# Expert down weights as one 4 MB transfer in 32 KB pieces, and their operand turned by half-identity products

## Chip, cores and metric

One core of a Trainium2 chip runs the whole kernel. The metric is the device time of one execution in microseconds, median of several; lower is better.

## The reference, cut to what matters

One encoder layer over 384 tokens (256 prompt frames and 8 x 16 sample frames) of width 2048, all in f32: an adaLN projection, a combined input projection, sliding-window attention beside gated linear attention, an output projection, and then a mixture of experts, in which the change lies. Each token goes to 2 of 32 experts with a hidden width of 512:

```python
def expert_block(args):
    xblk, e = args
    return (jax.nn.silu(xblk @ w_eg[e]) * (xblk @ w_eu[e])) @ w_ed[e]
```

`w_eg[e]` and `w_eu[e]` are 2048 x 512, `w_ed[e]` is 512 x 2048; each is 4 MB, so an expert has 12 MB and all of them 384 MB. Every expert's weights are read once, whatever its number of tokens. Each token's row is the sum of its two experts' results with their gates; it is scaled, added to x and normalised at the end.

## The kernel before, in words

The engines run programs of their own and meet at counting semaphores. Everything is written out by hand; the order on each engine is the order of its text.

**The ring.** Weights go through `ring`, 12 units of 8 KB per partition (1 MB each). For an expert, units 0 to 3 hold the gate weights, 4 to 7 the up weights, 8 to 11 (from `PRE` = 8) the down weights. SP loads them in six transfers of two units (2 MB, `unit_pair`), in the order gate, up, down (`expert`, L413 to L430). Each waits until `unit_used` says that TensorE has used the same two units of the expert before: TensorE adds 1 to it for each unit. A partition gets one contiguous piece of 16 KB in each transfer: `eg_v`, `eu_v` (8 neighbouring rows of 2 KB) and `ed_v` (`c=2`: two neighbouring rows of 8 KB). Expert 0's up units are requested early (L436), its gate and down units as the stages before leave the ring.

**An expert on TensorE** (`two_experts`, two experts per turn of the loop, buffers by `u`): `up(u, e)` takes the gate and the up product (L1260), in units 0 to 7, each f32 product on a half of the columns (`64 * q`), for 64 slots; it waits for `loaded[j]` at each pair of units (`expert_landed`). Then `rows_T` (L1243) turns the gathered rows of expert e + 1 by eight transposes; it waits for their gather. `hidden_T` (L1269) turns the hidden values of expert e by two 128 x 128 transposes into `bank[4]`, and ScalarE copies them to `hidT` (L1573, in `y_copy`). `down(u, e)` (L1283) takes the down product in units 8 to 11, 8 products of 512 columns for each two units, and adds 1 to `unit_used` after each unit. In this profile a product is two records.

**Beside it.** ScalarE computes the exponential of the gate, VectorE the rest of SwiGLU (L2057 to L2060); both copy the turned rows out of PSUM (L1561, L2052) and, after the down product, its result to `ysb` (L1576, L2065). GpSimd (`expert_rows`) waits for that copy, issues the scatter of expert e's result rows (L637, to `y_rows`), and then the gather of the rows of expert e + 2 (L632, into `xg`, read by `rows_T` one expert ahead). Both are indirect DMAs on GpSimd's own queue, one after the other, of 4 KB rows, 128 to a DMA; slots that hold no token are out of bounds and move nothing. They run on the same 16 DMA engines as the weights. After the last expert, `y_rows` is read back and the final norm follows.

An expert's hidden feature f lies in `hid` at partition (q, slot), f = 256 q + position. `hidden_T` before takes every second position (c = 0, 1), so that the partition p of unit 8 + 2q + c meets the weight row 256 q + 2p + c. This is the part that depends on how the rows of `w_ed` lie over the partitions.

Of the kernel before, what the change touches and what calls it, by code (L numbers as in the profile page):

```python
# [20 lines left out]
P = 128  # L21
D = 2048
# [8 lines left out]
NE, GRP, EPG = 32, 4, 8  # L31
# [10 lines left out]
PRE = 8  # L42
# [5 lines left out]
U_MOE = U_OUT + 16  # L48
UE = 12
# [52 lines left out]
def encoder_step(nc, A, O):  # L102
    with ExitStack() as ctx:
# [7 lines left out]
        ring = sb("ring", [P, RING * D])  # L111
        xbuf = sb("xbuf", [P, NT * D])
        hbuf = sb("hbuf", [P, KC * TOK])
# [11 lines left out]
        ident = sb("ident", [P, P])  # L125
# [24 lines left out]
        bank = [ctx.enter_context(nc.psum_tensor(f"bank{i}", [P, QN], F32)) for i in range(8)]  # L150
# [9 lines left out]
        def unit_pair(s):  # L160
            return ring[:, s * D:(s + 2) * D]

        arena = ring[:, PRE * D:RING * D]
        x = xbuf[:, :].rearrange("p (t d) -> p t d", t=NT)
        vr = xbuf[:, :].rearrange("p (a t c) -> p a t c", a=2, t=NT)
# [73 lines left out]
               for u in range(2)]  # L239
        ysb = [zbuf[:, 4096 + 1024 * u:5120 + 1024 * u] for u in range(2)]  # L240
        sg = [hbuf[:, 256 * u:256 * u + 256] for u in range(2)]
        hid = [hbuf[:, 512 + 256 * u:768 + 256 * u] for u in range(2)]
        hidT = [hbuf[:, 1024 + 256 * u:1280 + 256 * u].rearrange("p (c q s) -> p c q s", c=2, q=2)
                for u in range(2)]
        gfin = hbuf[:, 2048:4096]
        yk = [ring[:, 4096 * t:4096 * t + 4096].rearrange("p (k d) -> p k d", k=2) for t in range(NT)]
# [3 lines left out]
        loaded = [sem(f"loaded{s}") for s in range(RING)]  # L250
        unit_used, ada_used = sem("unit_used"), sem("ada_used")
# [46 lines left out]
        out_v = w_out.rearrange("(k p) c -> p k c", p=P)  # L298
        eg_v = A["w_expert_gate"][0].rearrange("e (g p c) f -> p e g (c f)", g=2, c=8)
        eu_v = A["w_expert_up"][0].rearrange("e (g p c) f -> p e g (c f)", g=2, c=8)  # L300
        ed_v = A["w_expert_down"][0].rearrange("e (q p c) d -> p e q (c d)", q=2, c=2)
        st_v = A["state_gla"][0].rearrange("b h k v -> b k h v")
        so_v = O["gla_state_sample"][0].rearrange("b h k v -> b k h v")
        yout = [O["y_prompt"][0, 0:P, :], O["y_prompt"][0, P:2 * P, :],
# [40 lines left out]
        def _(sp):  # L345
# [41 lines left out]
            for g in range(4):  # L387
                for j in range(8):
                    m, u = j // 4, j % 4
# [6 lines left out]
            for i in range(28):  # L396
                n = U_T + i
# [15 lines left out]

            def expert(e, first):

                for j in (0, 2, 8, 10) if first else range(0, UE, 2):
                    if first:
                        if j < 4:
                            last = max(n for n in range(U_MOE) if w_slot(n) in (j, j + 1))
                            sp.wait_ge(unit_used, last + 1)  # L420
                        elif j == PRE:
                            sp.wait_ge(h2_v, 12)
                            sp.wait_ge(h2_out[1], 16)
                        else:
                            sp.wait_ge(h2T_ps, 8)
                            sp.wait_ge(h2_out[0], 16)
                    else:
                        sp.wait_ge(unit_used, U_MOE + UE * (e - 1) + j + 2)
                    half_v = (eg_v, eu_v, ed_v)[j // 4][:, bass.ds(e, 1), j % 4 // 2, :]
                    sp.dma_start(unit_pair(j), half_v.rearrange("p e f -> p (e f)")).then_inc(loaded[j], 16)  # L430

            for j in (4, 6):
# [10 lines left out]
            with sp.If(n_over > 0):  # L443
                with sp.Fori(0, n_over) as i:
                    e = sp.value_load(ov_i[0:1, bass.ds(i + 1, 1)], min_val=0, max_val=NE - 1)
                    for j in range(0, UE, 2):
                        sp.wait_ge(unit_used, U_MOE + UE * (NE - 1) + UE * i + j + 2)
                        half_v = (eg_v, eu_v, ed_v)[j // 4][:, bass.ds(e, 1), j % 4 // 2, :]
                        sp.dma_start(unit_pair(j), half_v.rearrange("p e f -> p (e f)")).then_inc(loaded[j], 16)
            with sp.Else():  # L450
                sp.nop()
# [253 lines left out]
        def _(pe):  # L705
# [538 lines left out]
                last.then_inc(eT_ps, 1)  # L1244

            def expert_landed(j, e):
                j -= j % 2
                pe.wait_ge(loaded[j], 16 * loads[j] + 16 + e * 16)

            def up(u, e, t_need):  # L1250
# [13 lines left out]

            def hidden_T(u, e):
                pe.wait_ge(hid_sb, e + 1)
                units = hid[u].rearrange("p (n c) -> p c n", c=2)
                for c in range(2):
                    last = tr(bank[4][:, c * P:(c + 1) * P], units[:, c, :], ident[:, :])  # L1269
                last.then_inc(hT_ps, 1)  # L1270

            def down(u, e):

                pe.wait_ge(hT_sb, e + 1)
                if isinstance(e, int) and e == 0:
                    pe.wait_ge(ov_rdy, 1)
                wait_count(pe, y_v, e)
                wait_count(pe, y_a, e)
                for k in range(4):
                    expert_landed(8 + k, e)  # L1280
                    for n in range(2):
                        for q in range(2):
                            last = mm(bank[5 + n][64 * q:64 * q + 64, :], hidT[u][:, k % 2, k // 2, :],  # L1283
                                      unit(8 + k)[:, 1024 * q + QN * n:1024 * q + QN * n + QN],
                                      start=(k == 0), stop=(k == 3))
                    last.then_inc(unit_used, 1)
# [26 lines left out]
        def _(act):  # L1313
# [256 lines left out]

            def y_copy(u, e, sct_need):
                act.wait_ge(hT_ps, e + 1)
                cp(hidT[u].rearrange("p c q s -> p (c q s)"), bank[4][:, 0:256]).then_inc(hT_sb, 1)  # L1573
                act.wait_ge(unit_used, U_MOE + UE + e * UE)
                wait_count(act, sct[u], sct_need)
                cp(ysb[u][:, QN:2 * QN], bank[6][:, :]).then_inc(y_a, 1)  # L1576
# [610 lines left out]
```

## Time and profile before

| | us |
|---|---|
| median of 3 runs | 1856.45 (1856.37 to 1859.54) |
| the profiled execution, its own time | 1859.65 |
| its span | 1858.0 |
| TensorE busy | 1562.1 (84%) |
| VectorE, ScalarE, GpSimd busy | 393.5, 201.3, 181.9 |
| moved by DMA | 610.93 MB, mean 329 GB/s |
| 64 transfers each of gate, up and down weights, median to landing | 25.3, 26.7, 22.9 |

How to read it: the span is the time between the first and the last instruction of the profiled execution; its own time is the device's, and lies a little above. The expert stage runs from about 817 us, where the first gate product starts, to 1792 us. In the timeline, a row's number in brackets is how long the engine stood idle before it, and what released it.

### The profile page before, as it was taken

Reading aid. Unit: us, or ns where it says so; the run is one execution under the profiler, and the core shown is the slowest. Engines: PE = TensorE matmul, PEld = TensorE weight load, DVE = VectorE, ACT = ScalarE, POOL = GpSimd, SP = SyncE. Lnnn points to the kernel's source line nnn. Section 1 sums busy time; section 2 is a strip of 40 time slices with the busy share of each in tenths; the row PEclk is TensorE's granted clock in tenths of the full one; section 3 lists DMA queues with packets and bytes.
Section 4 is the critical chain, followed back from the end, with each engine's and each line's share of the span. In section 5 each row is a group of like instructions: output and inputs, shape, how many; then the busy total and the mean of one; then the engine's idle time right before and its main releaser. Section 6 shows DMA issues by size and latency. Waiting matters only on the chain.

```text
span 1858.0 us, 21570 instructions
## 1 busy us (share of the span) xinstructions
PE 1562.1 (84%) x8849; PEld 806.4 (43%) x8849; DVE 393.5 (21%) x852; ACT 201.3 (11%) x504; POOL 181.9 (10%) x372
## 2 busy tenths in 40 slices
PE   5999999999999999968798877777787888787840
PEld 2455444444454444554444434444444344444410
DVE  2012322224251311441111111101011111111115
ACT  3001111111221000200000000000000000000013
POOL 1031000000101020031010101010000011010102
PEclk9999999999999999978998999999989899999975
DMA  9998767666514593399999999999999999999952
GB/s 364 375 307 306 283 263 291 268 243 262 181 55 126 177 245 123 157 310 428 425 428 427 427 427 427 428 426 424 426 421 423 422 427 425 426 423 426 419 220 93
DMA packets 101954, 610.93 MB, mean 329 GB/s; under 512 B 15949, under 2 KB 18109, under 8 KB 65929
## 3 DMA queue, kind: packets, MB, share of 16 engines
q1 hardware_dynamic: 84242, 562.29, 74.8%
q0 software_dynamic: 16848, 41.68, 7.4%
q10 hardware_dynamic: 816, 6.29, 0.8%
q8 instruction: 34, 0.56, 0.1%
q14 instruction: 14, 0.11, 0.0%
HBM read 603.03 MB, written 28.40 MB: 340 GB/s over the span
## 4 chain that ended last, share of the span: by engine, by line
PE 49%; DMA 43%; DVE 3%; POOL 1%; issue 1%; ACT 1%; SPq 0%; POOLq 0%; DVEq 0%; ACTq 0%
DMA ring<-in_w_expert_up 36%; PE bank L823 9%; PE bank L1123 7%; PE bank L819 7%; PE bank L1260 6%; DMA zbuf<-h_rows,cur 5%; PE bank L1283 3%; PE bank L777 3%; PE bank L764 3%; PE bank L1150 2%; PE bank L743 1%; PE bank L768 1%; DMA ring<-in_w_ada 1%; DMA ring<-in_w_in 1%; DVE ring L2152 1%
## 5 line engine op out<-in xcount | busy, mean ns | idle before, releaser
L1260 PE MATMUL bank<-ring,zbuf 128*64 128x256 f32 x4096 | 464.2, 383 | 84.2 <-DMA ring<-in_w_expert_up 75.3
L1260 PEld LDWEIGHTS bank<-ring,zbuf 128*64 128x64 f32 x4096 | 291.5, 138 | 264.7 <-DMA ring<-in_w_expert_up 95.8
L1283 PE MATMUL bank<-ring,hbuf 128*64 128x512 f32 x1024 | 269.0, 685 | 17.6 <-ACT hbuf L1573 17.6
L823 PE MATMUL bank<-ring,hbuf 128*128 128x512 f32 x384 | 174.2, 599 | 2.9 <-ACT xbuf L1366 2.6
L1283 PEld LDWEIGHTS bank<-ring,hbuf 128*64 128x64 f32 x1024 | 82.3, 158 | 184.6 <-issue 182.7
L819 PE MATMUL bank<-hbuf,ring 128*128 128x384 f32 x384 | 133.8, 495 | 1.2 <-ACT zbuf L1362 0.8
L1123 PE MATMUL bank<-ring,zbuf 128*128 128x512 f32 x288 | 127.0, 595 | 3.1 <-DVE ring L1881 1.9
L2057 DVE TENSOR_SCALAR hbuf<-hbuf 128x256 f32<-128x256 f32 x32 | 9.4, 294 | 524.7 <-ACT hbuf L1565 524.7
L823 PEld LDWEIGHTS bank<-ring,hbuf 128*128 128x128 f32 x384 | 70.2, 190 | 83.7 <-issue 82.7
L819 PEld LDWEIGHTS bank<-hbuf,ring 128*128 128x128 f32 x384 | 69.8, 190 | 52.5 <-issue 11.0
L641 POOL CAST cur<-stab 128x1 int32 (+1 forms) x32 | 5.8, 181 | 861.5 <-DVE zbuf L2065 861.5
L1243 PE MATMUL bank<-ident,zbuf 128*128 128x128 f32 x264 | 43.2, 313 | 51.4 <-DMA zbuf<-h_rows,cur 51.4
L1123 PEld LDWEIGHTS bank<-ring,zbuf 128*128 128x128 f32 x288 | 53.7, 190 | 68.8 <-issue 68.7
L2065 DVE COPY zbuf<-bank 128x512 f32<-128x512 f32 x32 | 22.1, 692 | 286.8 <-PE bank L1283 286.8
L1565 ACT ACTIVATE hbuf<-bank 128x256 f32<-128x256 f32 x32 | 12.3, 384 | 523.1 <-PE bank L1260 523.1
L1243 PEld LDWEIGHTS bank<-ident,zbuf 128*128 128x128 f32 x264 | 35.2, 198 | 65.2 <-DMA zbuf<-h_rows,cur 60.6
L777 PE MATMUL bank<-ring,dbuf 128*32 128x512 f32 x512 | 59.1, 596 | 0.0
L2058 DVE RECIPROCAL hbuf<-hbuf 128x256 f32<-128x256 f32 x32 | 56.1, 1753 | 1.1
L1269 PE MATMUL bank<-ident,hbuf 128*128 128x128 f32 x64 | 17.9, 369 | 45.1 <-DVE hbuf L2060 45.0
L764 PE MATMUL bank<-hbuf,ring 128*128 128x384 f32 x128 | 50.3, 516 | 3.3 <-DMA ring<-in_w_in 3.3
L1576 ACT COPY zbuf<-bank 128x512 f32<-128x512 f32 x32 | 18.8, 586 | 275.5 <-PE bank L1283 275.5
L743 PE MATMUL bank<-ring,dbuf 128*32 128x512 f32 x256 | 39.3, 690 | 5.5 <-DMA ring<-in_w_ada 4.5
(389 smaller groups left out, 1133.4 us busy)
## 6 DMA issues: line engine op xcount, KB each, us to landing
ring<-in_w_expert_up SPq DMA_DIRECT2D x64, 2048.0 KB, 26.7
ring<-in_w_expert_gate SPq DMA_DIRECT2D x64, 2048.0 KB, 25.3
ring<-in_w_expert_down SPq DMA_DIRECT2D x64, 2048.0 KB, 22.9
ring<-in_w_ada SPq DMA_DIRECT2D x96, 1024.0 KB, 7.7
ring<-in_w_in SPq DMA_DIRECT2D x32, 1024.0 KB, 9.0
ring<-in_w_out SPq DMA_DIRECT2D x16, 1024.0 KB, 5.2
ring<-y_rows ACTq DMA_DIRECT2D x3, 2048.0 KB, 12.2
xbuf<-in_x_prompt SPq DMA_DIRECT2D x4, 1024.0 KB, 5.9
```

Source lines behind the costliest of these rows:

```text
L743: last = mm(bank[7][32 * q:32 * q + 32, :], cT[:, 4 * u + q, :], w[:, q, :], start=(u == 0), stop=(u == 3))
L764: last = mm(bank[c][:, 0:TOK], wq[:, k % 4, c * P:(c + 1) * P], hT[:, k, :], start=(k == 0), stop=(k == KC - 1))
L777: last = mm(bank[b][32 * q:32 * q + 32, :], cT[:, k, :], w[:, q * QN:(q + 1) * QN], start=(k == 0), stop=(k == KC - 1))
L819: last = mm(bank[c][:, 0:TOK], w[:, kk_, c * P:(c + 1) * P], hT[:, k, :], start=(k == 0), stop=(k == KC - 1))
L823: last = mm(bank[t][:, :], hT[:, k, t * P:(t + 1) * P], w[:, kk_, :], start=(k == 0), stop=(k == KC - 1))
L1123: last = mm(bank[3 * (b % 2) + t][:, :], zT[:, k, t * P:(t + 1) * P], w[:, i % 4, :], start=(k == 0), stop=(k == KC - 1))
L1150: last = mm(bank[3 + t][:, :], zT[:, k, t * P:(t + 1) * P], w[:, k % 4, :], start=(k == 0), stop=(k == KC - 1))
L1243: last = tr(bank[c // 4][:, (c % 4) * P:(c % 4 + 1) * P], rows[:, c, :], ident[:, :])
L1260: last = mm(bank[2 + u][64 * q:64 * q + 64, 256 * (j // 4):256 * (j // 4) + 256], xeT[u][:, k % 8, k // 8, :], w[:, kk_, 256 * q:256 * q + ...
L1283: last = mm(bank[5 + n][64 * q:64 * q + 64, :], hidT[u][:, k % 2, k // 2, :], unit(8 + k)[:, 1024 * q + QN * n:1024 * q + QN * n + QN], st ...
L2058: link(v.reciprocal(sg[u], sg[u]))
L2065: cp(ysb[u][:, 0:QN], bank[5][:, :]).then_inc(y_v, 1)
```

## The change

`ed_v` takes four neighbouring rows per partition (`c=4`), so that the down weights of an expert lie as 32 KB contiguous per partition, and one transfer loads all four units (`whole`, 4 MB). SP requests it when all 12 units of the expert before are used; it stays behind the up units in the order. `expert_landed` asks for the one semaphore before each of the four down units. Partition p of unit 8 + c now holds row 4p + c, so for hidden half q its 64 x 4 features must stand on partitions 64 q to 64 q + 63: `hidden_T` becomes eight products (4 c, 2 q) with half an identity as the moving operand, 64 columns each, with output at partition 64 q of `bank[4]`. `hidT` keeps its size and its copy. The same goes for the loop over overflowing experts.

```diff
--- before.py
+++ after.py
@@ -160,6 +160,9 @@
         def unit_pair(s):
             return ring[:, s * D:(s + 2) * D]
 
+        def whole(s):
+            return ring[:, s * D:(s + 4) * D]
+
         arena = ring[:, PRE * D:RING * D]
         x = xbuf[:, :].rearrange("p (t d) -> p t d", t=NT)
         vr = xbuf[:, :].rearrange("p (a t c) -> p a t c", a=2, t=NT)
@@ -240,7 +243,7 @@
         ysb = [zbuf[:, 4096 + 1024 * u:5120 + 1024 * u] for u in range(2)]
         sg = [hbuf[:, 256 * u:256 * u + 256] for u in range(2)]
         hid = [hbuf[:, 512 + 256 * u:768 + 256 * u] for u in range(2)]
-        hidT = [hbuf[:, 1024 + 256 * u:1280 + 256 * u].rearrange("p (c q s) -> p c q s", c=2, q=2)
+        hidT = [hbuf[:, 1024 + 256 * u:1280 + 256 * u].rearrange("p (c s) -> p c s", c=4)
                 for u in range(2)]
         gfin = hbuf[:, 2048:4096]
         yk = [ring[:, 4096 * t:4096 * t + 4096].rearrange("p (k d) -> p k d", k=2) for t in range(NT)]
@@ -298,7 +301,7 @@
         out_v = w_out.rearrange("(k p) c -> p k c", p=P)
         eg_v = A["w_expert_gate"][0].rearrange("e (g p c) f -> p e g (c f)", g=2, c=8)
         eu_v = A["w_expert_up"][0].rearrange("e (g p c) f -> p e g (c f)", g=2, c=8)
-        ed_v = A["w_expert_down"][0].rearrange("e (q p c) d -> p e q (c d)", q=2, c=2)
+        ed_v = A["w_expert_down"][0].rearrange("e (p c) d -> p e (c d)", c=4)
         st_v = A["state_gla"][0].rearrange("b h k v -> b k h v")
         so_v = O["gla_state_sample"][0].rearrange("b h k v -> b k h v")
         yout = [O["y_prompt"][0, 0:P, :], O["y_prompt"][0, P:2 * P, :],
@@ -413,7 +416,7 @@
 
             def expert(e, first):
 
-                for j in (0, 2, 8, 10) if first else range(0, UE, 2):
+                for j in (0, 2, 8) if first else (0, 2, 4, 6, 8):
                     if first:
                         if j < 4:
                             last = max(n for n in range(U_MOE) if w_slot(n) in (j, j + 1))
@@ -421,12 +424,14 @@
                         elif j == PRE:
                             sp.wait_ge(h2_v, 12)
                             sp.wait_ge(h2_out[1], 16)
-                        else:
                             sp.wait_ge(h2T_ps, 8)
                             sp.wait_ge(h2_out[0], 16)
                     else:
-                        sp.wait_ge(unit_used, U_MOE + UE * (e - 1) + j + 2)
-                    half_v = (eg_v, eu_v, ed_v)[j // 4][:, bass.ds(e, 1), j % 4 // 2, :]
+                        sp.wait_ge(unit_used, U_MOE + UE * (e - 1) + (UE if j == PRE else j + 2))
+                    if j == PRE:
+                        sp.dma_start(whole(j), ed_v[:, bass.ds(e, 1), :].rearrange("p e f -> p (e f)")).then_inc(loaded[j], 16)
+                        continue
+                    half_v = (eg_v, eu_v)[j // 4][:, bass.ds(e, 1), j % 4 // 2, :]
                     sp.dma_start(unit_pair(j), half_v.rearrange("p e f -> p (e f)")).then_inc(loaded[j], 16)
 
             for j in (4, 6):
@@ -443,9 +448,12 @@
             with sp.If(n_over > 0):
                 with sp.Fori(0, n_over) as i:
                     e = sp.value_load(ov_i[0:1, bass.ds(i + 1, 1)], min_val=0, max_val=NE - 1)
-                    for j in range(0, UE, 2):
-                        sp.wait_ge(unit_used, U_MOE + UE * (NE - 1) + UE * i + j + 2)
-                        half_v = (eg_v, eu_v, ed_v)[j // 4][:, bass.ds(e, 1), j % 4 // 2, :]
+                    for j in (0, 2, 4, 6, 8):
+                        sp.wait_ge(unit_used, U_MOE + UE * (NE - 1) + UE * i + (UE if j == PRE else j + 2))
+                        if j == PRE:
+                            sp.dma_start(whole(j), ed_v[:, bass.ds(e, 1), :].rearrange("p e f -> p (e f)")).then_inc(loaded[j], 16)
+                            continue
+                        half_v = (eg_v, eu_v)[j // 4][:, bass.ds(e, 1), j % 4 // 2, :]
                         sp.dma_start(unit_pair(j), half_v.rearrange("p e f -> p (e f)")).then_inc(loaded[j], 16)
             with sp.Else():
                 sp.nop()
@@ -1244,7 +1252,7 @@
                 last.then_inc(eT_ps, 1)
 
             def expert_landed(j, e):
-                j -= j % 2
+                j = min(j - j % 2, PRE)
                 pe.wait_ge(loaded[j], 16 * loads[j] + 16 + e * 16)
 
             def up(u, e, t_need):
@@ -1264,9 +1272,11 @@
 
             def hidden_T(u, e):
                 pe.wait_ge(hid_sb, e + 1)
-                units = hid[u].rearrange("p (n c) -> p c n", c=2)
-                for c in range(2):
-                    last = tr(bank[4][:, c * P:(c + 1) * P], units[:, c, :], ident[:, :])
+                units = hid[u].rearrange("p (n c) -> p c n", c=4)
+                for c in range(4):
+                    for q in range(2):
+                        last = mm(bank[4][64 * q:64 * q + 64, 64 * c:64 * c + 64], units[:, c, :], ident[:, 64 * q:64 * q + 64],
+                                  start=True, stop=True)
                 last.then_inc(hT_ps, 1)
 
             def down(u, e):
@@ -1280,7 +1290,7 @@
                     expert_landed(8 + k, e)
                     for n in range(2):
                         for q in range(2):
-                            last = mm(bank[5 + n][64 * q:64 * q + 64, :], hidT[u][:, k % 2, k // 2, :],
+                            last = mm(bank[5 + n][64 * q:64 * q + 64, :], hidT[u][:, k, :],
                                       unit(8 + k)[:, 1024 * q + QN * n:1024 * q + QN * n + QN],
                                       start=(k == 0), stop=(k == 3))
                     last.then_inc(unit_used, 1)
@@ -1570,7 +1580,7 @@
 
             def y_copy(u, e, sct_need):
                 act.wait_ge(hT_ps, e + 1)
-                cp(hidT[u].rearrange("p c q s -> p (c q s)"), bank[4][:, 0:256]).then_inc(hT_sb, 1)
+                cp(hidT[u].rearrange("p c s -> p (c s)"), bank[4][:, 0:256]).then_inc(hT_sb, 1)
                 act.wait_ge(unit_used, U_MOE + UE + e * UE)
                 wait_count(act, sct[u], sct_need)
                 cp(ysb[u][:, QN:2 * QN], bank[6][:, :]).then_inc(y_a, 1)
```

## Rows read from the trace of the kernel before

**Rows 1.** The page: the span in 40 slices, GB/s of the DMA engines, and the chain that ended last

```profile
GB/s 364 375 307 306 283 263 291 268 243 262 181 55 126 177 245 123 157 310 428 425 428 427 427 427 427 428 426 424 426 421 423 422 427 425 426 423 426 419 220 93
...
DMA ring<-in_w_expert_up 36%; PE bank L823 9%; PE bank L1123 7%; PE bank L819 7%; PE bank L1260 6%; DMA zbuf<-h_rows,cur 5%; PE bank L1283 3%; PE bank L777 3%; PE bank L764 3%; PE bank L1150 2%; PE bank L743 1%; PE bank L768 1%; DMA ring<-in_w_ada 1%; DMA ring<-in_w_in 1%; DVE ring L2152 1%
```

**Rows 2.** Windows: length, busy us (instructions) of each engine, PEclk, DMA share, GB/s

```profile
0.00:100.00 100.00, 80.84 (x429) 38.82 (x433) 18.73 (x42) 20.53 (x34) 6.70 (x40) 0.97 1.02 371
...
850.00:852.00 2.00, 2.00 (x22) 1.26 (x18) 0.00 (x0) 0.00 (x0) 1.76 (x4) 1.00 1.03 442
...
1000.00:1200.00 200.00, 157.54 (x1130) 85.70 (x1126) 28.77 (x41) 12.82 (x27) 17.57 (x37) 0.96 1.01 427
1200.00:1400.00 200.00, 156.58 (x1118) 83.15 (x1116) 25.79 (x37) 12.16 (x25) 19.66 (x42) 0.97 1.00 425
```

**Rows 3.** Waits of TensorE, 860 to 1060 us: total, times, longest

```profile
PE bank L1243 <- DMA zbuf<-h_rows,cur: 27.1, 7, 5.0
...
PE bank L1260 <- DMA ring<-in_w_expert_up: 1.3, 1, 1.3
```

**Rows 4.** Waits of TensorE, 1080 to 1780 us

```profile
PE bank L1260 <- DMA ring<-in_w_expert_up: 71.5, 42, 2.4
...
PE bank L1243 <- DMA zbuf<-h_rows,cur: 11.6, 9, 2.4
```

**Rows 5.** Timeline of TensorE: start, us, instructions; last pair of up units, experts 13 and 31

```profile
1221.62 3.67 PE L1260 MATMUL bank<-ring,zbuf 128*64 128x256 f32 x32 [1.92 <-DMA ring<-in_w_expert_up]
...
1773.84 3.67 PE L1260 MATMUL bank<-ring,zbuf 128*64 128x256 f32 x32 [1.82 <-DMA ring<-in_w_expert_up]
```

**Rows 6.** Timeline of TensorE, 840 to 1046 us, the early experts

```profile
840.45 7.84 PE L1283 MATMUL bank<-ring,hbuf 128*64 128x512 f32 x32 [0.52 <-ACT hbuf L1573]
...
866.88 1.97 PE L1243 MATMUL bank<-ident,zbuf 128*128 128x128 f32 x8 [4.77 <-DMA zbuf<-h_rows,cur]
...
868.65 0.63 PE L1269 MATMUL bank<-ident,hbuf 128*128 128x128 f32 x2
...
869.80 8.52 PE L1283 MATMUL bank<-ring,hbuf 128*64 128x512 f32 x32 [0.52 <-ACT hbuf L1573]
...
1045.31 5.22 PE L1283 MATMUL bank<-ring,hbuf 128*64 128x512 f32 x12 [0.54 <-ACT hbuf L1573]
```

**Rows 7.** Timeline of SP and GpSimd, 801 to 852 us, their DMA issues

```profile
801.34 0.80 SPq L430 DMA_DIRECT2D ring<-in_w_expert_down  x2
...
844.90 3.77 SPq L430 DMA_DIRECT2D ring<-in_w_expert_down  x2
...
849.79 1.03 POOL L637 DMA_INDIRECT y_rows<-zbuf,cur  x1 [0.23 <-issue]
...
851.44 1.05 POOL L632 DMA_INDIRECT zbuf<-h_rows,cur  x1 [0.15 <-issue]
851.94 3.77 SPq L430 DMA_DIRECT2D ring<-in_w_expert_gate  x2
```

**Rows 8.** DMA issues and us to landing: 844:850, 849:853, 1755:1761, 1790:1800

```profile
ring<-in_w_expert_down SPq DMA_DIRECT2D x2, 2048.0 KB, 13.0
...
y_rows<-zbuf,cur POOLq DMA_INDIRECT x1, 10.2
zbuf<-h_rows,cur POOLq DMA_INDIRECT x1, 15.4
...
ring<-in_w_expert_down SPq DMA_DIRECT2D x2, 2048.0 KB, 24.1
...
y_rows<-zbuf,cur POOLq DMA_INDIRECT x1, 2.9
```

**Rows 9.** DMA queues, 1500 to 1760 us: packets, MB, share

```profile
q0 software_dynamic: 2336, 3.37, 3.5%
```

**Rows 10.** Timeline, the last expert: SP's issue and the down product

```profile
1755.61 3.77 SPq L430 DMA_DIRECT2D ring<-in_w_expert_down  x2
...
1782.26 9.67 PE L1283 MATMUL bank<-ring,hbuf 128*64 128x512 f32 x32 [0.54 <-ACT hbuf L1573]
```

## The prediction

> **What bounds the kernel now.** I read the stages first. From slice 18 of 40 on, the page's row of GB/s stands at about 427, and the longest item in the chain of waits is the landing of expert weights [rows 1]. The windows say the same: between 1000 and 1400 us the DMA engines are busy for 1.00 of the time at 425 to 427 GB/s, while TensorE is busy for 157 of 200 us [rows 2]. The expert stage is about half of the span and all of the change lies in it.
>
> Then I asked whether the weights set the pace in all of it. The waits of TensorE say no. Between 860 and 1060 us it waits 27.1 us in 7 waits for gathered rows (`rows_T`, L1243) and 1.3 us for weights [rows 3]. Between 1080 and 1780 us it is the other way: 71.5 us before the up products alone for weights, 11.6 us for rows [rows 4]. So there are two regimes. Expert 0's weights lie in the ring before its rows exist, so TensorE starts with a full ring and paces itself; it is a little faster than the DMA engines and catches up with them after some seven experts.
>
> The two paces. While the weights bind, TensorE reaches the last pair of up units at 1221.62 us and, 18 experts later, at 1773.84 us: 552.2/18 = **30.68 us an expert** [rows 5]. While TensorE paces itself, the down product starts at 869.80 and at 1045.31 us, six experts apart: 175.5/6 = **29.25 us** [rows 6]. The margin is only 1.4 us.
>
> What the 29.25 us hold: the down product of expert 0 ends at T = 840.45 + 7.84 = 848.3. GpSimd issues the scatter at 849.79 and the next gather at 851.44, on one queue [rows 7]. They land 10.2 and 15.4 us later, the gather thus at 866.8 [rows 8]; `rows_T` starts at 866.88, having waited 4.77 us, and the down product follows at 869.80 [rows 6]. The loop is down product, scatter, gather, `rows_T`, `hidden_T`, down product. **The gather's landing sets it**, not arithmetic: up(e) is finished when it comes.
>
> What makes the gather slow. Alone on idle DMA engines the last scatter lands 2.9 us after its issue; beside the weights it takes 10.2 [rows 8]. The 7.3 us between are time given to weight pieces. One 16 KB piece takes 16 x 16384 B / 427 GB/s = 0.614 us on its engine [rows 2], so some 12 weight pieces pass. Sixteen gathers and scatters make 2336 packets on the software queue [rows 9]: 2336/16 DMAs/16 engines = 9 an engine for each. So about one weight piece passes before each small packet, and a few more in front of the first.
>
> **The change, part by part.**
>
> *One 4 MB transfer.* Each engine gets 8 pieces of 32 KB (8 partitions) where it had 16 of 16 KB. The bytes are the same: 9.82 us at 427 GB/s. SP issues one DMA fewer, which is worth nothing: a transfer issued 24.1 us before it lands [rows 8] isn't held by its issue.
>
> *The later issue.* Today the halves of down(e+1) are issued when half and all of down(e) are used: 844.90 and 848.3 (two issues in 3.77 us) [rows 7]. After, both go at the end. Queued behind that wait on SP are the gate units of the next expert, whose own condition comes 3.5 us after that (851.94, [rows 7]), so they lose nothing. Does the queue run dry? The pair lands on average 13.0 us after issue [rows 8]. With one taking 4.9 us and the issues 3.4 apart, they land at about 857.2 and 862.0, so the first began near 851: the new issue at 848.5 and some 1.5 us of start are in time, by under 1 us. Price of this part alone: 0 to 2 us, once; I take 0. The first expert's merged wait costs nothing, since both halves are issued there within 0.8 us (two issues at 801.34, [rows 7]).
>
> *The down product waits for all of its weights.* In the steady state they land about 2 us after `hidden_T` is done; TensorE makes it up in the gate product, since it waits 71.5/42 = 1.7 us before each pair of up units [rows 4]. At the end the last pair, issued at 1755.61 and 3.4 us later [rows 10], lands on average 24.1 us after issue [rows 8], so both by about 1784; the last down product starts at 1782.26. Cost 0 to 2 us; with the next part I take 1.
>
> *`hidden_T` as eight half-identity products.* Two transposes take 0.63 us while TensorE paces itself [rows 6]. Every f32 product shows as two records (4096 for 2048), so eight make 16. At most they run at the pace of the 128*64 records of L1260, 3.67/32 = 0.115 us [rows 5]: 1.84 us and a pipe end of 0.3, so +1.5. At least they stream a quarter of that column count: 16 x 0.03 + 0.3, so +0.2. I take **+0.9 us**. It lies in the loop above; the copy by ScalarE behind it keeps its size. While the weights bind it is hidden by their pace (30.68 against 30.15 us); without that cover it counts in full, and so it stands in the sum.
>
> *The 32 KB piece beside the gather.* No row shows one. If it can't be interrupted, each one ahead of or between the small packets holds them 0.61 us longer. When TensorE paces itself the down transfer is issued 0.2 us after T, the scatter 1.5 us and the gather 3.1 us after T, so they run together. All eight delay the chain: 8 x 0.61 = 4.9 us. None: 0. Some are gone before the scatter's first packet stands in the queue: I count one for the 1.3 us between the issues, one under way and one for the start of the software queue, and take five: **+3.1 us**.
>
> **The sum.** 29.25 + 0.9 + 3.1 = 33.25 us an expert. That is more than 30.68, so TensorE never catches up; the DMA queue runs empty before each down product ends, the next down transfer starts with it, and it meets the scatter and gather again. What was a phase of seven experts holds for all. From the end of the first down product (848.3 + 0.9) 31 experts take 31 x 33.25 = 1030.8 us, ending at 1880.0; before it was 1782.26 + 9.67 = 1791.9 [rows 10]. The difference is 88 us. What follows keeps its length. The profiled execution took 1859.65 us, 3.2 over the median of the runs, 1856.45; the sum becomes 1948 against the first and **1945 us** against the median.
>
> A rule of the Trainium skill ("DMA: Bandwidth & Descriptors", section "Queues, rings and completion order") bears on the five: it says that an engine takes turns between its queues by whole packets of some 9 to 17 descriptors and not by single ones. By it one expert transfer's share on an engine would be one turn, which is the first rival below. No row read here shows the order of single packets; the sum goes by single pieces (+3.1 us an expert), by the page's rule it would be +4.9.
>
> **The rivals.**
>
> *A turn is a whole transfer.* Each engine would finish all eight pieces of a transfer before it serves the other queue. The 7.3 us of the scatter are 1.5 shares of 4.9 us, which doesn't speak against it. The share of the down transfer becomes 9.8 us, the gather is later by the full 4.9, the loop is 35.05 us, and the end is 0.9 + 31 x 35.05 - 943.6 = +144 us: 2000 us.
>
> *The piece isn't carried as 32 KB* (the change does not do what it says), or small packets pass through it. Then the loop is 29.25 + 0.9 = 30.15 us, still below 30.68, the weights bind again, later than before, and only the end shows: 0.9 + 1 and at most 1 for the start, 1859 us. The point between this and the forecast is a delay of the gather by 0.5 us an expert. For it: no row has a piece above 16 KB. Against it: 16 KB pieces are not passed through.
>
> *Faster.* Longer pieces move faster and the gather isn't late. Place: the down transfer. In short windows the engines reach 442 GB/s [rows 2]; a down transfer at that rate would take 9.49 us for 9.82, 31 x 0.33 = 10 us less, with 2.5 given back at the ends: 1849 us. It decides from 436 GB/s on (0.2 us an expert, 6.2 in all: 2.5 for the ends and 3.7 to be seen). For it: the first 100 us, with pieces of 2 KB mostly, show 371 GB/s at full engines. That is 2 KB in 88 ns and 16 KB in 614, so about 13 ns a piece beside its bytes. But 8 pieces fewer give only 0.1 us an expert, 3 us in all. Against it: the delay of the gather must then stay under 0.5 us.
>
> **Chances.** The forecast's mechanism 0.70, with an own range of 1904 (31.95 us: +0.3 and +2.4) to 1990 (34.7 us: +1.5 and +3.95). The whole turn 0.05, no delay 0.17, faster 0.08. A measurement of this kernel can tell 0.2% (3.7 us) from no change. The third case divides into 0.12 within that and 0.05 beyond it: faster 0.08, same 0.12, slower 0.80. The range reaches from 1858 (takes in the case without delay) to 1990; it leaves out the whole turn, the faster case and some tails, not over 0.2.
>
> **What would show it.** If right: waits of L1243 for gathered rows in nearly every expert, 7 to 9 us each, to the end; waits of L1260 for weights gone; the down product starting every 33 us; the gather landing after 17 to 19 us and the down transfer after 12 to 13, for 24.1 in the steady state; windows at 1000 to 1400 us with a DMA share near 0.92 and about 393 GB/s. `hidden_T` alone shows in L1269: 1.2 to 1.8 us. Wrong: a DMA share that stays 1.00 and an expert every 30.7 us (no delay), or every 35 us (whole turn); packets that don't fall by 128 an expert (no 32 KB pieces); a share of 1.00 with more than 436 GB/s (faster). If the gather is late but L1269 is short, the 0.9 was the wrong term; if TensorE catches up after more experts, the five pieces were too many.

## The result and the profile after

The changed kernel takes 1940.01 us (median of 4 runs, 1935.6 to 1943.5) against 1857.66 for the kernel before in the same comparison: ratio **1.044, 95% interval 1.0419 to 1.046**, slower. Forecast were 1945 us and a range of 1858 to 1990. The two profiled executions took 1940.11 and 1859.65 us, 80.5 apart, and nearly all of it lies in the expert stage: the last down product ends at 1863.72 + 8.78 = 1872.5 us, where it ended at 1791.9 [rows 10].

The page of the changed kernel: DMA busy tenths and GB/s by slice, then the two large queues (packets, MB, share of 16 engines).

```profile
DMA  9998767757224853799999999899999999999952
GB/s 366 382 297 312 282 261 282 282 226 260 84 73 146 256 150 152 266 363 387 398 383 388 403 382 407 368 410 376 411 372 394 386 397 390 390 412 394 405 203 108
...
q1 hardware_dynamic: 79634, 562.29, 72.4%
q0 software_dynamic: 16848, 41.68, 7.0%
```

The bytes are the same, and the slices that stood at 427 GB/s [rows 1] now lie between 368 and 412. The weight queue has 84242 - 79634 = 4608 packets fewer: 32 x 128 weight pieces and 32 x 16 completion packets. The 32 KB pieces are real (a transfer adds 16 small packets to its pieces, here called completion packets; the run with one late transfer below shows them alone). The chain that ended last:

```profile
DMA zbuf<-h_rows,cur 27%; PE bank L1293 15%; PE bank L831 9%; PE bank L1131 7%; PE bank L827 6%; PE bank L1251 3%; PE bank L785 3%; PE bank L772 2%; PE bank L1158 2%; PE bank L1278 2%; PE bank L751 1%; DVE zbuf L2075 1%; PE bank L776 1%; POOL y_rows L645 1%; DMA ring<-in_w_ada 1%
```

Its longest item was the landing of expert weights, 36% [rows 1]; now it is the landing of gathered rows. Windows (as in [rows 2]):

```profile
1000.00:1200.00 200.00, 154.42 (x1104) 85.89 (x1104) 27.16 (x39) 11.56 (x24) 16.77 (x36) 0.85 0.94 393
1200.00:1400.00 200.00, 155.21 (x1104) 86.09 (x1104) 25.83 (x37) 11.56 (x24) 16.78 (x36) 0.85 0.94 393
```

The DMA engines have 6% of idle time where they had none, 393 GB/s for 427 [rows 2]. Waits of TensorE from 860 to 1060 us, then from 1080 to 1860 us:

```profile
PE bank L1251 <- DMA zbuf<-h_rows,cur: 42.8, 6, 8.2
```

```profile
PE bank L1251 <- DMA zbuf<-h_rows,cur: 155.4, 23, 7.9
PE bank L1293 <- ACT hbuf L1583: 12.6, 23, 0.5
```

No wait for weights is left in the later stage, where there were 42 before up products [rows 4]. The wait for gathered rows, 27.1/7 = 3.9 us on average in the early experts and nearly gone later (11.6 us in 9 waits) [rows 3, 4], is now 42.8/6 = 7.1 us in the early and 155.4/23 = 6.8 us in the later ones. One turn of the loop, with the down products of experts 1, 30 and 31 around it:

```profile
877.44 7.09 PE L1293 MATMUL bank<-ring,hbuf 128*64 128x512 f32 x32 [0.47 <-ACT hbuf L1583]
...
1237.21 1.97 PE L1251 MATMUL bank<-ident,zbuf 128*128 128x128 f32 x8 [6.79 <-DMA zbuf<-h_rows,cur]
...
1239.11 1.23 PE L1278 MATMUL bank<-ident,hbuf 128*64 128x64 f32 x16
...
1240.88 9.63 PE L1293 MATMUL bank<-ring,hbuf 128*64 128x512 f32 x32 [0.55 <-ACT hbuf L1583]
...
1250.35 13.98 PE L1268 MATMUL bank<-ring,zbuf 128*64 128x256 f32 x128
...
1250.56 0.33 SPq L432 DMA_DIRECT2D ring<-in_w_expert_down  x1
...
1252.29 1.01 POOL L645 DMA_INDIRECT y_rows<-zbuf,cur  x1 [0.32 <-issue]
...
1253.92 1.04 POOL L640 DMA_INDIRECT zbuf<-h_rows,cur  x1 [0.15 <-issue]
...
1271.05 1.98 PE L1251 MATMUL bank<-ident,zbuf 128*128 128x128 f32 x8 [6.72 <-DMA zbuf<-h_rows,cur]
...
1835.28 9.39 PE L1293 MATMUL bank<-ring,hbuf 128*64 128x512 f32 x32 [0.55 <-ACT hbuf L1583]
...
1863.72 8.78 PE L1293 MATMUL bank<-ring,hbuf 128*64 128x512 f32 x32 [0.55 <-ACT hbuf L1583]
```

From 877.44 to 1835.28 us are 29 experts: **33.03 us an expert**, where there were 29.25 in the early phase and 30.68 later [rows 5, 6]. The order can be read off: the down product ends at about 1250.4, the 4 MB transfer is requested at 1250.56, the scatter at 1252.29, the gather at 1253.92; the gate and up products are done at 1264.3, and TensorE stands idle for 6.7 us until the rows are there. DMA issues from 860 to 1800 us, median us to landing:

```profile
ring<-in_w_expert_down SPq DMA_DIRECT2D x28, 4096.0 KB, 13.1
...
y_rows<-zbuf,cur POOLq DMA_INDIRECT x28, 13.3
zbuf<-h_rows,cur POOLq DMA_INDIRECT x28, 17.2
```

The down weights land 13.1 us after their request, as the pair did in the early experts before (13.0 [rows 8]); the gather takes 17.2 us and the scatter 13.3.

The packets that start in short windows show how the two queues share the engines: around this turn's request from 1249.5 to 1251.4 us, then from 1251.4 to 1256.9 and from 1257.65 to 1262 us; last, the kernel before from 1243.9 to 1252 us, beside its scatter and gather.

```profile
DMA packets 1, 0.00 MB, mean 0 GB/s; under 512 B 1, under 2 KB 1, under 8 KB 1
...
q1 hardware_dynamic: 64, 2.10, 101.3%
...
q1 hardware_dynamic: 51, 1.67, 89.0%
q0 software_dynamic: 50, 0.15, 8.6%
...
q1 hardware_dynamic: 216, 3.13, 90.7%
q0 software_dynamic: 213, 0.35, 11.5%
```

In the changed kernel the weight queue is empty when the down transfer is requested. Then 64 pieces of 32 KB start, four an engine, before the first packet of the scatter, though the scatter was issued at 1252.29. From there on the queues take turns nearly one for one, single weight pieces against single small packets: 51 to 50 with 32 KB pieces, 216 to 213 in the kernel before.

### The profile page after: what moved, and what is told of

It is laid out like the page before. It is cut to its first block, busy times and chain, and to the rows that moved or that the text cites. A ratio compares the mean times of both kernels' runs of the same rounds, so it can differ in the third digit from the quotient of the medians.

```text
span 1938.5 us, 22372 instructions
## 1 busy us (share of the span) xinstructions
PE 1603.9 (83%) x9297; PEld 848.7 (44%) x9297; DVE 395.3 (20%) x852; ACT 201.8 (10%) x504; POOL 181.0 (9%) x372
## 3 DMA queue, kind: packets, MB, share of 16 engines
q1 hardware_dynamic: 79634, 562.29, 72.4%
## 4 chain that ended last, share of the span: by engine, by line
PE 58%; DMA 29%; DVE 4%; POOL 3%; issue 3%; ACT 1%; SPq 0%; POOLq 0%; DVEq 0%
DMA zbuf<-h_rows,cur 27%; PE bank L1293 15%; PE bank L831 9%; PE bank L1131 7%; PE bank L827 6%; PE bank L1251 3%; PE bank L785 3%; PE bank L772 2%; PE bank L1158 2%; PE bank L1278 2%; PE bank L751 1%; DVE zbuf L2075 1%; PE bank L776 1%; POOL y_rows L645 1%; DMA ring<-in_w_ada 1%
## 5 line engine op out<-in xcount | busy, mean ns | idle before, releaser
L1268 PE MATMUL bank<-ring,zbuf 128*64 128x256 f32 x4096 | 449.1, 380 | 0.8 <-DVE zbuf L2062 0.8
L1293 PE MATMUL bank<-ring,hbuf 128*64 128x512 f32 x1024 | 280.7, 710 | 17.4 <-ACT hbuf L1583 17.4
L1251 PE MATMUL bank<-ident,zbuf 128*128 128x128 f32 x264 | 64.1, 421 | 217.0 <-DMA zbuf<-h_rows,cur 217.0
L1251 PEld LDWEIGHTS bank<-ident,zbuf 128*128 128x128 f32 x264 | 51.1, 219 | 231.7 <-DMA zbuf<-h_rows,cur 231.7
L2075 DVE COPY zbuf<-bank 128x512 f32<-128x512 f32 x32 | 22.1, 691 | 314.9 <-PE bank L1293 314.9
L785 PE MATMUL bank<-ring,dbuf 128*32 128x512 f32 x512 | 59.1, 596 | 0.0
L2062 DVE COPY zbuf<-bank 128x512 f32<-128x512 f32 x33 | 22.8, 691 | 174.0 <-PE bank L1251 174.0
L1586 ACT COPY zbuf<-bank 128x512 f32<-128x512 f32 x32 | 18.7, 585 | 287.4 <-PE bank L1293 287.4
L1571 ACT COPY zbuf<-bank 128x512 f32<-128x512 f32 x33 | 19.3, 586 | 273.9 <-PE bank L1251 273.9
## 6 DMA issues: line engine op xcount, KB each, us to landing
ring<-in_w_expert_down SPq DMA_DIRECT2D x32, 4096.0 KB, 13.1
```

The lines of the kernel that those rows point to most:

```text
L785: last = mm(bank[b][32 * q:32 * q + 32, :], cT[:, k, :], w[:, q * QN:(q + 1) * QN], start=(k == 0), stop=(k == KC - 1))
L1251: last = tr(bank[c // 4][:, (c % 4) * P:(c % 4 + 1) * P], rows[:, c, :], ident[:, :])
L1268: last = mm(bank[2 + u][64 * q:64 * q + 64, 256 * (j // 4):256 * (j // 4) + 256], xeT[u][:, k % 8, k // 8, :], w[:, kk_, 256 * q:256 * q + ...
L1293: last = mm(bank[5 + n][64 * q:64 * q + 64, :], hidT[u][:, k, :], unit(8 + k)[:, 1024 * q + QN * n:1024 * q + QN * n + QN], start=(k == 0) ...
L2075: cp(ysb[u][:, 0:QN], bank[5][:, :]).then_inc(y_v, 1)
```

## The experiments

All ran beside the kernel before; ratios are to it, with 95% intervals. The code of an edit is cut to its core. The changed kernel was run once more, unchanged: 1942.48 us, 1.0433 (1.0415 to 1.045), DMA share 0.94 again.

> The changed kernel once more, unchanged, beside the run above on the same chip: 1935 to 1943 us, loop 33.0 us.

### Only the size of a piece

The 4 MB as two transfers of 2 MB, requested together at the late moment. Each takes two of the four rows of every partition, so a piece is 16 KB.

```diff
-sp.dma_start(whole(j), ed_v[:, bass.ds(e, 1), :]...).then_inc(loaded[j], 16)
+for h in range(2):
+    sp.dma_start(unit_pair(j + 2 * h), ed_v[:, bass.ds(e, 1), 2 * D * h:2 * D * (h + 1)]...).then_inc(loaded[j], 16)
```

> The changed kernel, but the 4 MB are asked for as two 2 MB transfers of 16 KB pieces, one after the other, at the same late moment, with the same rows per partition and one semaphore. Only the size of a piece differs. Theory (32 KB pieces hold up the gather): the gather lands after 15.4 us again, the expert loop falls to 29.9 us or so, below 30.68, the weights bind again after the first experts, 1857 to 1866 us. Rival (the late request makes the weight queue run dry): no change, 1940 us, DMA share 0.93. Rival (the eight products): no change either, 1940 us.

Measured: 1866.69 us, 1.0038 (1.0023 to 1.0052). Its windows from 850 and from 1000 us, its DMA issues from 1080 to 1300 us, and TensorE's wait for rows from 860 to 1060 us:

```profile
850.00:1000.00 150.00, 123.84 (x914) 70.90 (x912) 21.29 (x30) 9.57 (x20) 14.01 (x30) 0.87 1.00 416
1000.00:1200.00 200.00, 170.54 (x1241) 95.04 (x1238) 28.14 (x39) 12.52 (x26) 19.57 (x42) 0.88 1.01 425
...
y_rows<-zbuf,cur POOLq DMA_INDIRECT x7, 10.3
zbuf<-h_rows,cur POOLq DMA_INDIRECT x7, 14.1
...
PE bank L1253 <- DMA zbuf<-h_rows,cur: 31.1, 7, 5.8
```

The gather lands after 14.1 us again, the DMA engines are full again, and some 75 of the 82 us are gone. Late request and products are all there, so without the 32 KB pieces they don't bring the loss, alone or together. Some 6 us stay: from 850 to 1000 us the queues move 416 GB/s for 427 (11 GB/s over 150 us are 1.65 MB, or 3.9 us at 427), where the early experts run at TensorE's pace with the slower products and the later request; the rest was not taken apart.

### One transfer, but 16 KB pieces

The kernel before with the down weights as one late 4 MB transfer. The old rows per partition give two separate pieces of 16 KB on each; the two transposes stay.

```diff
-sp.dma_start(unit_pair(j), half_v...)                       # two halves
+sp.dma_start(whole(j).rearrange("p (q f) -> p q f", q=2), ed_v[:, bass.ds(e, 1), :, :]...)   # "e (q p c) d -> p e q (c d)"
```

> The kernel before with one change: the down weights as one 4 MB transfer, requested when all units are used, but with the old rows per partition, so two separate pieces of 16 KB on each, and the two transposes. Theory: 1857 to 1862 us (0 to 2 us at the start, 0 to 2 us at the end), expert period 30.68 us. Rival (late request): most of the 82 us, 1920 to 1940 us. Rival (the products): 1857 us.

Measured: 1862.53 us, 1.0009 (0.9997 to 1.0021). Its windows from 850 and from 1000 us, its DMA issues from 1080 to 1300 us, and the weight queue on its page:

```profile
850.00:1000.00 150.00, 122.92 (x856) 68.04 (x854) 21.36 (x30) 9.15 (x20) 14.09 (x31) 0.89 1.01 426
1000.00:1200.00 200.00, 163.58 (x1119) 89.25 (x1116) 28.52 (x40) 11.37 (x25) 17.47 (x37) 0.86 1.00 424
...
y_rows<-zbuf,cur POOLq DMA_INDIRECT x7, 10.7
zbuf<-h_rows,cur POOLq DMA_INDIRECT x7, 14.7
```

```profile
q1 hardware_dynamic: 83730, 562.29, 74.9%
```

A 4 MB transfer of 16 KB pieces does no harm, though its share on an engine is as long as the changed kernel's: the gather lands after 14.7 us. The queue's packets fell only by the 512 completion packets. **What counts is the piece, not the transfer.** This refutes the rival by whole turns (2000 us), as do the packet counts above: a turn is a single piece. So the rule of the Trainium skill ("DMA: Bandwidth & Descriptors", "Queues, rings and completion order", turns of some 9 to 17 descriptors) doesn't describe what the gather met here.

The same split on the changed kernel's own rows, where the two pieces lie one behind the other, was joined again: 79634 packets, as in the changed kernel, and 1936.18 us, 1.041 (1.0374 to 1.0446). It tells nothing new of the pieces, only that writing a pattern in two parts doesn't cut it.

> The changed kernel, one 4 MB transfer as there, its access pattern written as two pieces of 16 KB on each partition that lie one behind the other. Theory: if the pattern is kept, packets are 16 KB (256 an expert) and the time is 1860 to 1867 us; if it is joined again, packets are 32 KB and the time is that of the changed kernel, 1940 us. Rival (one transfer of 4 MB, whatever its pieces, is one turn on each engine): 1940 us with 256 packets of 16 KB.

### Only the products

16 KB pieces in halves at the old moments; the new rows per partition and the eight products stay.

> The changed kernel with the down weights in halves of 2 MB and 16 KB pieces, requested at the old moments; the rows per partition and the eight products stay. Theory: the products cost 0.75 us an expert only while TensorE sets the pace, and 1 us at the end: 1857 to 1861 us, expert period 30.68 us in the later stage. Rival (the products): 31 x 0.75 = 23 us over the kernel before, 1880 us. Rival (late request): 1857 to 1861 too.

Measured: 1862.40 us, 1.0011 (1.0001 to 1.0021): 2 us. While the weights bind, the products are hidden. The other way round, the changed kernel with the two old transposes (it leaves out the new order of the features, so its result is another one; the amounts of work are the same):

```diff
-for c in range(4):
-    for q in range(2):
-        last = mm(bank[4][64 * q:64 * q + 64, 64 * c:64 * c + 64], units[:, c, :], ident[:, 64 * q:64 * q + 64], ...)
+for c in range(2):
+    last = tr(bank[4][:, c * P:(c + 1) * P], units[:, c, :], ident[:, :])
```

> The changed kernel with the two old transposes in place of the eight products; the down product then multiplies the wrong features (the result of the experts is left wrong, all amounts of work are the same). Theory: the products are one term of the loop, 0.6 to 0.75 us an expert: 31 times that off, 1917 to 1922 us, and the loop 32.3 to 32.5 us, still over 30.68. Rival (the products are what tips the loop over): 1857 to 1866 us. Rival (late request): as the theory.

Measured: 1910.84 us, 1.0285 (1.0266 to 1.0304); 29 us less than the changed kernel's 1940, its loop 32.07 us (906.14 to 1803.98 us, 28 experts). Its waits of TensorE from 1080 to 1760 us:

```profile
PE bank L1251 <- DMA zbuf<-h_rows,cur: 152.5, 21, 9.7
```

So the products cost 1.0 us an expert inside the loop, above the 0.6 to 0.75 expected, which makes them some 29 of the 82 us once the loop binds. They are not what tips it over: with the transposes it stays above 30.68.

### Cutting the loop

The gather one expert earlier on GpSimd, all of the change kept: behind the scatter of expert e it now fetches the rows of expert e + 3. (Cut: one more gather before the loop, one more column in its table, one more wait at its end.)

```diff
-wait_count(pool, eT_ps, 2 * i + u)
-column(gcur[:, 1 - u, :], gtab, 2 * i + (u + 1))
-gather(gcur[:, 1 - u, :], 1 - u)
+pool.wait_ge(eT_ps, 2 * i + (u + 1))
+column(gcur[:, u, :], gtab, 2 * i + (u + 2))
+gather(gcur[:, u, :], u)
```

> The changed kernel with the gather of each expert's rows one expert earlier on GpSimd (the rows of expert 1 before the loop, then those of e + 2 where those of e + 1 were; one more gather at the end, never read). 32 KB pieces, late request and eight products stay. Theory (the loop down product, scatter, gather, turned rows): the loop is cut, TensorE needs 14 + 4 + 2 + 8.5 = 28.5 to 29 us an expert, the weights bind at 30.7 and the time is 1857 to 1866 us, with no waits for gathered rows. Rival (32 KB pieces are slow for the weights themselves, or the queue runs dry at each expert): the waits go over to the weights and 1920 to 1940 us stay.

Measured: 1860.73 us, 1.0011 (0.9997 to 1.0025). Its waits of TensorE from 1080 to 1760 us, and its DMA issues from 1080 to 1300 us:

```profile
PE bank L1281 <- DVE hbuf L2074: 53.3, 22, 2.4
PE bank L1296 <- DMA ring<-in_w_expert_down: 47.1, 23, 2.6
PE bank L1271 <- DMA ring<-in_w_expert_up: 11.7, 17, 1.3
```

```profile
y_rows<-zbuf,cur POOLq DMA_INDIRECT x7, 14.9
zbuf<-h_rows,cur POOLq DMA_INDIRECT x7, 18.9
```

The gather is slower than ever, 18.9 us, and costs nothing, because nobody waits for it: the slow loop is not the slow gather alone but the gather as a link between two down products. The 32 KB pieces don't harm the weights themselves. In the kernel before, the same edit:

> The kernel before with the gather one expert earlier, and nothing else. Theory: the weights bind nearly the whole stage already, so only the end can gain: 1855 to 1861 us, same. Rival (the gather costs time in the kernel before too): 11.6 + 27 us of waits go, down to 1825 us.

Measured: 1861.55 us, 1.0007 (0.9995 to 1.002), no difference. Its DMA issues in the same window:

```profile
y_rows<-zbuf,cur POOLq DMA_INDIRECT x7, 10.3
zbuf<-h_rows,cur POOLq DMA_INDIRECT x7, 14.2
```

With 16 KB pieces the gather lands after 14.2 us; the 32 KB pieces make it 4.7 us longer, near the bound of eight times half a piece (8 x 0.61 = 4.9). By the trace's packet records 6.6 of the eight, on average over the engines, start between the first small packet of the scatter and the last of the gather. The gather waits of the kernel before were free, as its weights bind. None of these versions beats the kernel before.

### 8 KB pieces

As the first run, with four transfers of 1 MB.

> The changed kernel with the down weights as four 1 MB transfers of 8 KB pieces at the same late moment. Theory, by piece size: an 8 KB piece holds an engine 0.31 us, so the gather that meets the down weights lands about as much earlier than with 16 KB as that does than with 32 KB, up to 3 us: 12 to 13.5 us after its issue in the early experts; the time stays with the weights, 1860 to 1866 us. Rival (what counts is a transfer's whole share on an engine, not the piece): as with 16 KB, 14.6 us.

Measured: 1867.23 us, 1.0037 (1.0024 to 1.005). Its DMA issues from 1080 to 1300 us:

```profile
y_rows<-zbuf,cur POOLq DMA_INDIRECT x7, 9.8
zbuf<-h_rows,cur POOLq DMA_INDIRECT x7, 11.4
```

The gather lands after 11.4 us, a little under the 12 to 13.5 expected (11.0 in the early experts): 8, 16 and 32 KB give 11.4, 14.1 and 17.2 (in the loop) or 18.9 us (with the gather ahead). The time is no better, as the weights bind; the 7 us more fit a weight rate of 422 GB/s for 425 and the later request, which were not separated.

### Does a lead keep the loop off?

The forecast reasoned that the loop sets in because TensorE paces the early experts. So experts 1 to 15 got halves of 16 KB pieces at the old moments and experts 16 to 31 the 32 KB pieces at the late one. The first try asked for them as two transfers of 64 partitions.

> Experts 1 to 15 as in the run with products alone (16 KB pieces, halves at the old moments); from expert 16 on 32 KB pieces at the late moment (as two transfers of 64 partitions each, 4 pieces an engine in each). By then the weights have begun to set the pace and the weight queue has some 18 us of lead. Theory A (the loop needs TensorE's pace to start it; with a lead the down weights do not meet the scatter and the gather): 1861 to 1868 us, later experts at 30.7 us. Theory B (the later request and the 32 KB pieces use the lead up, and the loop sets in within some experts): later experts at 33 us, up to 16 x 2.4 = 38 us more, 1880 to 1900 us.

Measured: 2058.19 us, 1.1062 (1.104 to 1.1083). Windows before and after the switch:

```profile
1000.00:1200.00 200.00, 173.61 (x1228) 102.89 (x1226) 26.32 (x37) 12.16 (x25) 19.58 (x42) 0.85 1.00 422
...
1500.00:1700.00 200.00, 121.13 (x848) 73.43 (x850) 18.47 (x26) 9.27 (x19) 13.98 (x30) 0.76 0.96 310
```

Here the transfers are slow in themselves: DMA share 0.96, but 310 GB/s. By the packet records a 32 KB piece takes 2.5 us on its engine (median, 1500 to 1700 us), in the changed kernel 1.2. The run tells nothing of the lead; a 64-partition transfer was a change of its own. The second try has the whole transfer.

> The question of the run before without its second change (its transfers of 64 partitions moved at 310 GB/s): experts 1 to 15 with 16 KB pieces in halves at the old moments, from expert 16 on the whole 4 MB transfer of the changed kernel, 32 KB pieces on all 128 partitions at the late moment. Theory A (with some 18 us of lead on the weight queue the down weights meet neither scatter nor gather, and the weights go on setting the pace): 1861 to 1868 us, no gather waits of 6 to 7 us. Theory B (the lead is used up within a few experts and the loop sets in): up to 16 x 2.35 = 38 us more, 1880 to 1900 us, gather waits near 6.7 us and an expert every 33 us in the last ten.

Measured: 1896.18 us, 1.0178 (1.0162 to 1.0195); the loop set in with the first changed expert. But there was little lead at the switch: the down weights had landed 16.7 us after their request, in the kernel before 24.0. The third has the two transposes too (and so again another result) and the full lead.

> The run before once more with the two transposes in place of the eight products (the down product multiplies the wrong features, the amounts of work are the same). In the run before, TensorE with the products had gained no lead by expert 16: the down weights landed 16.7 us after their request, in the kernel before 24. Here they should land 22 to 24 us after it when the switch to 32 KB pieces and the late request comes. Theory A (a full lead keeps the loop off): 1860 to 1868 us, later experts at 30.7 us. Theory B (the lead is used up all the same): the loop of the changed kernel with transposes, 32.1 us, sets in after some experts: 1872 to 1886 us, gather waits of 6 to 9 us at the end.

Measured: 1883.96 us, 1.0125 (1.0108 to 1.0142). The landing of its down weights from 1200, 1310, 1360 and 1500 us on:

```profile
ring<-in_w_expert_down SPq DMA_DIRECT2D x6, 2048.0 KB, 22.7
ring<-in_w_expert_down SPq DMA_DIRECT2D x1, 4096.0 KB, 23.6
...
ring<-in_w_expert_down SPq DMA_DIRECT2D x1, 4096.0 KB, 18.9
...
ring<-in_w_expert_down SPq DMA_DIRECT2D x1, 4096.0 KB, 14.4
...
ring<-in_w_expert_down SPq DMA_DIRECT2D x7, 4096.0 KB, 13.5
```

and the wait for gathered rows from 1500 to 1780 us:

```profile
PE bank L1258 <- DMA zbuf<-h_rows,cur: 67.0, 9, 8.6
```

The lead falls from 22.7 us (16 KB) over 23.6 and 18.9 to 14.4 within three experts, and then the loop stands, 31.85 us an expert (1361.93 to 1807.86, 14 experts). The lead doesn't even keep the 32 KB pieces away from the gather: at the first changed expert, with the weights landing after 23.6 us, the gather takes 20.5 us (14.2 before it) and TensorE waits 6.85 us for its rows. **The loop needs no start-up phase; it draws the kernel in from either side.**

## Why the prediction was right

**Which loop binds.** Right. The two regimes, read from the waits by window, were the whole case: a margin of 1.4 us between TensorE's own pace and the weights', and the gather's landing on the path. The run with the gather ahead shows that cutting this one link takes away the loss. Of the signs named in advance, three came out just beside their figures: waits of 6.8 us (7 to 9), down weights after 13.1 us (12 to 13), a DMA share of 0.94 (0.92).

**The gather beside 32 KB pieces**, forecast +3.1 us. The wait before the turned rows went from 3.9 to 6.8 us, +2.9; against the run with 16 KB pieces at the same moment it is 7.1 to 31.1/7 = 4.4 us between 860 and 1060 us, +2.7; the other 0.5 us, from 3.9 to 4.4, came with the late request and the products. The forecast let three of the eight pieces pass ahead and counted five. The packet records (1080 to 1800 us, averages over the engines) divide it otherwise: four start before the scatter's first packet and four among the small ones, 4 x 0.61 = 2.4 us, and that first packet comes 5.2 us after the issue for 4.5 before, +0.7. That makes 3.1 us too; the mechanism was right, and that the size fell on the same number was in part luck. The bound for all eight pieces, 4.9 us, is nearly met (4.7) with the gather ahead.

**The products**, forecast +0.9 us in the loop. Their records take 1.23 us for 0.63, and from the start of the turned rows to the down product it is 3.67 us for 2.92, +0.75. The run with transposes gives 1.0 us in all: the down product is shorter there too (mean record 667 ns for 710), and the wait for rows 0.5 us longer (152.5/21 = 7.3 for 6.8).

**The sum.** 29.25 + 2.9 + 0.75 = 32.9 for 33.03 measured and 33.25 forecast. Over the stage it is 80.5 us for 88, and the difference is made of three parts. The first 30 steps took 33.08 us each (842.92 to 1835.28), 5 us less in all. The last step took only 28.44 us (1835.28 to 1863.72), 4.8 less: no gate and up weights follow it, the last gather lands after 10.2 us, and nothing waits for it; the forecast charged the full loop there too. Against that, the first down product ended at 851.9 us and not at 849.2, 2.7 later.

**The later request and the wait for all weights**, forecast 0 and 1 us: the run with 16 KB pieces in one late transfer has +2 us with an interval that reaches to no change. In combination with the products (first run) it was 6 us, so the "under 1 us" in time for an empty queue was too narrow a margin to call it free. (The forecast's working lets the first half begin near 851 us; 857.2 - 4.9 is 852.3.) The 1 us for the end isn't in the forecast's sum of 88 us.

**The rivals.** Whole turns: refuted by the single 4 MB transfer of 16 KB pieces. Not carried as 32 KB: refuted by the packets. Faster: the weights gained nothing that can be seen; with the loop cut, the 32 KB pieces move 425 to 426 GB/s, as 16 KB ones do.

**What the forecast left open.** It said that the phase of seven experts "holds for all" because TensorE never catches up. That is true, but the last runs show more: had TensorE caught up, it would have been drawn back.

## What to carry to other kernels

A large contiguous piece is not free for its neighbours. Here the small packets of another queue passed between bulk pieces, nearly one for one, so that the gather's time grew with the piece (11.4, 14.1, 17.2 us for 8, 16, 32 KB), while going from 16 to 32 KB brought the bulk nothing (425 to 427 GB/s with either). Before enlarging pieces or delaying a bulk request, look for a small transfer that closes a loop (result, scatter, gather, next input) and for the margin of that loop to the bound that now hides it. Two cures worked here: pieces of 16 KB (1862 to 1867 us), or the small transfer one step earlier (1861 us), which took the loss away although that transfer had become slower.

## What the runs showed of the hardware that was not expected

Bulk transfers of 64 partitions keep the DMA engines busy at half the rate: with a third of the weight bytes in such transfers it is 310 GB/s on average, for 422 with 128 partitions throughout, and a 32 KB piece takes 2.5 us instead of 1.2. The Trainium skill ("SBUF — State Buffer", section "Door 1: The DMA port swizzle") states that partitions 0 to 63 reach only 8 of the 16 ports. The run agrees with it, by the doubled time of a piece; such a transfer was not measured alone.

Two contiguous pieces written as two parts of an access pattern go out as one of 32 KB (79634 packets either way).

TensorE's granted clock is lower in the slow loop, 0.85 for 0.96 between 1000 and 1200 us [rows 2], as a mean over stretches at 2.4 GHz (1.00, as from 1252 to 1262 us) and at 1.2 GHz (0.50, as from 1238 to 1239 us). Before `rows_T` it has stood idle for 6.3 to 8.2 us in experts 1 to 30, and those eight transposes take 1.97 us each time, where they took 1.16 to 1.97 in the kernel before; the down product takes up to 9.64 us for 7.09 in a stretch at full clock. Against the early experts before, from which the forecast starts, this adds little (the transposes took 1.16 to 1.97 us there, the down product 7.8 to 9.9). Nor is the clock the cause of the loss: the kernel with one late transfer of 16 KB pieces was granted 0.86 in the same window and lost nothing that can be told from noise.
